# RWKV's input columns by halves of its heads, the memory's stage beside the weights, and mLSTM's denominators as columns

## The reference

```python
n = rmsnorm(x, attn_norm);  u = n @ w_in                 # 6928 columns of weights
mix = concat(gated_deltanet(u_gdn), mlstm(u_mlstm), rglru(u_rglru), rwkv7(u_rwkv))
x = x + mix @ w_out
n = rmsnorm(x, ffn_norm);   x = x + (silu(n @ w_gate) * (n @ w_up)) @ w_down
# second block: the normed memory of 256 tokens gives keys and values for one of three attentions
mem_n = rms_norm(mem, norm_mem_g);  mkv = mem_n @ w_mem_kv
x = x + merged_attentions(rms_norm(x) @ w_in_2, mkv) @ w_out_2;  return rms_norm(x, norm_final_g)
```

## Time and profile before

| | |
|---|---|
| median of three runs | 2525.97 us (2525.31 to 2526.02) |
| the profiled execution | 2521.66 us, span 2519.9 us |
| TensorE busy | 2442.4 us, 97%, 14420 matmuls |
| VectorE busy | 1438.4 us, 57%, 1852 instructions |
| ScalarE busy | 1131.4 us, 45%, 1408 instructions |
| POOL busy | 101.8 us, 4%, 93 instructions |
| TensorE's granted clock, mean | 0.986 of full speed |

### The profile page before, as it was taken

How to read it: one execution, slowest core, us unless ns; L and a number is a source line. 1 busy time by engine, 2 the same in 40 slices (tenths; PEclk the granted TensorE clock), 3 DMA queues, 4 the chain that set the end, 5 groups by cost and what they waited for, 6 DMA issues and landing times. The chain is left out here.

```text
span 2519.9 us, 34232 instructions
## 1 busy us (share of the span) xinstructions
PE 2442.4 (97%) x14420; PEld 2079.4 (83%) x14420; DVE 1438.4 (57%) x1852; ACT 1131.4 (45%) x1408; POOL 101.8 (4%) x93
## 2 busy tenths in 40 slices
PE   8999979998999999999999999999999999999998
PEld 8888878987788888888888887888888888888887
DVE  4575754776675555555555576545445655555554
ACT  5442622554354344444444464445544455344444
POOL 2000000121000000000000023000000000000000
PEclk9999989999999999999999999999999999999999
DMA  7633313644455555555556556555545544555564
GB/s 250 218 118 101 121 65 102 227 139 171 144 194 196 184 189 193 184 186 184 189 185 194 187 180 227 193 184 167 176 157 180 188 151 134 200 190 194 184 235 149
DMA packets 219528, 441.51 MB, mean 175 GB/s; under 512 B 11922, under 2 KB 15856, under 8 KB 216944
## 3 DMA queue, kind: packets, MB, share of 16 engines
q1 hardware_dynamic: 215632, 419.80, 50.4%
q0 software_dynamic: 3744, 19.53, 2.0%
HBM read 428.81 MB, written 10.49 MB: 174 GB/s over the span
## 5 line engine op out<-in xcount | busy, mean ns | idle before, releaser
L1183 ACT CAST ringH<-raw 128x1024 fp32r<-128x1024 f32 (+1 forms) x784 | 817.6, 1046 | 1060.2 <-PE ps L577 901.5
L1736 DVE TENSOR_TENSOR ringL<-raw,ringH 128x1024 fp32r<-128x1024 f32 (+1 forms) x784 | 951.7, 1231 | 431.0 <-ACT ringH L1183 429.9
L575 PE MATMUL ps<-ringH,nS 128*128 128x512 f32 x1376 | 554.2, 403 | 4.2 <-DVE ringL L1736 3.9
L576 PE MATMUL ps<-ringL,nS 128*128 128x512 f32 x1376 | 538.4, 391 | 0.0
L577 PE MATMUL ps<-ringH,nS 128*128 128x512 f32 x1376 | 538.4, 391 | 0.0
L603 PE MATMUL ps<-nS,ringH 128*128 128x256 f32 x1056 | 318.0, 301 | 16.5 <-DVE ringL L1736 16.5
L575 PEld LDWEIGHTS ps<-ringH,nS 128*128 128x128 f32 x1376 | 260.0, 189 | 58.6 <-issue 4.9
L604 PE MATMUL ps<-nS,ringH 128*128 128x256 f32 x1056 | 306.8, 291 | 0.0
L605 PE MATMUL ps<-nS,ringL 128*128 128x256 f32 x1056 | 306.5, 290 | 0.0
L577 PEld LDWEIGHTS ps<-ringH,nS 128*128 128x128 f32 x1376 | 259.5, 189 | 55.8
L576 PEld LDWEIGHTS ps<-ringL,nS 128*128 128x128 f32 x1376 | 260.4, 189 | 49.2
(11 more groups left out here) (392 smaller groups left out, 2175.4 us busy)
## 6 DMA issues: line engine op xcount, KB each, us to landing
raw<-in_w_in SPq DMA_DIRECT2D x187, 1024.0 KB, 5.1
raw<-in_ffn_w_gate SPq DMA_DIRECT2D x44, 1024.0 KB, 5.2
raw<-in_ffn_w_up SPq DMA_DIRECT2D x44, 1024.0 KB, 5.2
raw<-in_ffn_w_down SPq DMA_DIRECT2D x44, 1024.0 KB, 5.2
raw<-in_w_out SPq DMA_DIRECT2D x32, 1024.0 KB, 5.2
raw<-in_w_mem_kv SPq DMA_DIRECT2D x16, 1024.0 KB, 5.2
raw<-in_w_proj_a SPq DMA_DIRECT2D x8, 1024.0 KB, 5.2
raw<-in_w_proj_m SPq DMA_DIRECT2D x8, 1024.0 KB, 5.1
```

What stands on the lines that cost most here:

```text
L575: mm(o, XH[:, ts(j)], WH, first, False)
L576: mm(o, XH[:, ts(j)], WL, False, False)
L1183: e.copy(ringH[:, h % NSPL, 0:nh * cols], raw[:, u % NRAW, h0 * cols:(h0 + nh) * cols]).then_inc(*hi.tick(h))
L1736: tt2(ringL[:, h % NSPL, o], raw[:, u % NRAW, h0 * cols:(h0 + nh) * cols], ringH[:, h % NSPL, o].bitcast(F32), SUB).then_inc(*lo.tick(h))
```

## The change

- The `w` blocks become seven of 256 columns. `w0` to `w3` hold the first four heads' r, k, v and the low-rank columns, `w4` to `w6` the second four heads'. Units and half units still hold 2048 and 1024 columns, so a unit is then 8 k tiles. `weave` counts a step by its columns.
- `norm` places one step per pair instead of two.
- `mem` no longer stands by itself ahead of `rwkv`: a generator `beside_rwkv` runs it with four steps after each piece until `w3` is done, and the rest of it beside `rwkv`; `mlstm` follows in the same generator from `m3` on. ScalarE squares the memory's tokens after the second and third pair instead of behind the eighth. The buffer `memSt` becomes two tiles elsewhere, `memk` moves, and ScalarE's drain of `m0` waits for the squares and the four holding DMAs; POOL zeroes `mU` behind those DMAs.
- The token shift goes by pairs of tiles (one subtraction for two). The second heads' r, k and v are shifted inside the first heads' scan, after `Z` of chunks 0 to 2.
- Paces in `rwkv` and `gdn` are raised.
- mLSTM: `den` becomes one column per token and head, by six one-column matmuls in place of the product with `ones`; `m_t` is turned once for all heads. The absolute value, the MAX and the reciprocal work on columns, and the division moves into the factor of the norm.

The diff, cut to its core:

```diff
 def weave(self, stage, n):
         for pace in stage:
             due += n if pace is None else pace
-            self.step(int(due))
-            due -= int(due)
+            while self.i < len(self.steps) and due >= self.steps[self.i].block.cols / 512:
+                cost, i = self.steps[self.i].block.cols / 512, self.i
+                self.step()
+                due -= cost
+                if self.i == i:
+                    due = 0.0
+def beside_rwkv(L):
+    yield from L.stage("mem")
+    while not L.done("m3"):
+        yield
+    yield from L.stage("mlstm")
 def course(L):
-    L.weave(L.stage("norm"), 2)
+    L.weave(L.stage("norm"), 1)
...
-    L.weave(L.stage("mem"), 3)
-    L.weave(L.both(L.stage("rwkv"), L.stage("mlstm"), "m3"), 1.5)
+    side = beside_rwkv(L)
+    while not L.done("w3"):
+        next(side)
+        L.step(4)
+    L.weave(L.both(L.stage("rwkv"), side, "w3"), 1.5)
...
-        for q in range(4):
-            block(f"w{q}", win[:, RWC + 512 * q:min(RWC + 512 * q + 512, 6928)], 16, 512 if q < 3 else 256, "x", by="V")
+        for q in range(7):
+            c = RWC + (512 * q if q < 4 else 512 * (q - 4) + 256)
+            block(f"w{q}", win[:, c:c + 256], 16, 256, "x", by="V")
# TensorE, rwkv
-                for _ in range(7):
-                    yield 1.3
+                for _ in range(4):
+                    yield 2.5
...
# behind V's turn
-                    yield 4 + hh
+                    yield 6 + 2 * hh
# behind the spread of kk
-                    yield 3 + 3 * hh
+                    yield 4 + 4 * hh
# behind tokB
-                    yield 3 + hh
+                    yield 3 + 2 * hh
-                    yield from invert(rw_p, rw_v, rw_a, (hh, "inv"), narrow, GT, X, XR, T1, 5, 1.3 + 0.5 * hh)
+                    yield from invert(rw_p, rw_v, rw_a, (hh, "inv"), narrow, GT, X, XR, T1, 5, 1.5 + 0.8 * hh)
# TensorE, mlstm, per head
-                    for n in range(2):
-                        t = m1(b[:, 256 * n:256 * n + 256], ident[:, h:h + 1].broadcast_to([128, 128]), grows[3 + n], n == 0)
+                    t = m1(b[:, 0:256], ident[:, h:h + 1].broadcast_to([128, 128]), grows[3], True)
# m_t, turned once for all heads
+                    if h == 0:
+                        for tt in range(2):
+                            t = m1(b[:, 256 + 4 * tt:260 + 4 * tt], grows[4][:, ts(tt)], ident[:, 0:4], False)
...
-                    for n in range(2):
-                        for s in range(2):
-                            l_ = ones if n else mV[:, s, ts(h)]
-                            t = m1(b[:, 256 * n + 128 * s:256 * n + 256], l_, S_[:, s, 128 * s:256], n == 0 and s == 0)
+                    for s in range(2):
+                        mm(b[:, 128 * s:256], mV[:, s, ts(h)], S_[:, s, 128 * s:256], s == 0, False)
+                    for s, tt in ((0, 0), (0, 1), (1, 1)):
+                        for c in range(2):
+                            o = 128 * tt + 64 * c
+                            t = m1(b[half(c), 256 + tt:257 + tt], S_[:, s, o:o + 64], ones[:, 0:1], False)
# TensorE, gdn: paces 9 -> 10, 8 -> 9, 3.5 -> 4, inversion 2.6 -> 3
# ScalarE
# drain
+                if tag == "m0":
+                    e.wait_ge(*me_a.at("ss", 1))
+                    for g in range(4):
+                        e.wait_ge(s_mh[g], 16)
...
# mem, behind the eighth pair
-                square(0)
-                square(1)
...
-                    act(Mb, ring.of("ml", "H", h)[:, 256:512], ACT.Abs).then_inc(*ml_a.tick("ab", h))
# VectorE, rwkv
-                for k in [12, 13, *range(12)]:
...
+                for n, k in enumerate((12, 0, 4, 8)):
+                    shift(k, v3(SC + 512 * (n % 2), 2, T))
+                    yield
...
# in the scan, behind Z of chunk c
+                        if hh == 0 and c < 3:
+                            own(rw_v)
+                            shift(4 * c + 2, u3(4))
# VectorE, mlstm, per head
-                    tt2(Mb, Mb, Eb, MAX).then_inc(*ml_v.tick())
-                    e.reciprocal(Mb, Mb).then_inc(*ml_v.tick())
-                    tt2(Mb, Mb, mix[:, 4 + h, :], MUL).then_inc(*ml_v.tick())
-                    tt2(mix[:, 4 + h, :], Mb, b[:, 0:256], MUL).then_inc(*ml_v.tick("t3", h))
+                    tt2(mix[:, 4 + h, :], mix[:, 4 + h, :], b[:, 0:256], MUL).then_inc(*ml_v.tick())
+                    d = den[:, 2 * h:2 * h + 2]
+                    e.tensor_copy(d, b[:, 256:258]).then_inc(*ml_v.tick())
+                    stt(out=d, in0=d, scalar=-1.0, in1=d, op0=MUL, op1=MAX).then_inc(*ml_v.tick())
+                    tt2(d, d, low_m[:, 2 * h:2 * h + 2], MAX).then_inc(*ml_v.tick("t3", h))
```

More of the change, by code:

```diff
@@ L372, in program @@
         assert XBo >= 8704 and XBo + 4096 <= SC and SGo >= SC + 9728 + 2 * T + 512, (XBo, SC, NAR)
-        mSt = alias("memSt", SC + 4096, [128, 2, 4, 2, T])
+        assert MU + 988 == GU + 4096 and MU + 988 + 2048 <= RU
+        mSt = [alias(f"memSt{k}", o, [128, 4, 2, T]) for k, o in enumerate((0, MU + 988))]
         gateS = alias("gateS", 0, [128, 4096])
@@ L391, in program @@
         rxb, rmb = v2(SC + 9728, T), v2(SC + 9728 + T, T)
+        den, low_m, den_inv = (small[:, o:o + 8] for o in (64, 72, 80))
         col_rw, col_gd, col_ml = small[:, 24:32], small[:, 88:104], small[:, 104:112]
@@ L1000, in gdn @@
                         t.then_inc(*gd_p.tick("ga", w, g))
-                        yield 3.5
-                yield from invert(gd_p, gd_v, gd_a, ("inv",), wide, G8, X8, XR8, T8, 5, 2.6)
+                        yield 4
+                yield from invert(gd_p, gd_v, gd_a, ("inv",), wide, G8, X8, XR8, T8, 5, 3)
                 yield from join(gd_p, gd_v, ("inv",), G8, X8, XR8, T8, 2.6)
@@ L1289, in unit, with to_rows @@
                     place_rope(blocks[s.block.n - 1].tag)
-            def to_rows(key, mp, ma, gain, put, held, square):
+            def to_rows(key, mp, ma, gain, put, held, square, turns):
                 for n in range(8):
@@ L1298, in to_rows, with squared @@
                         act(put(k), ring.of(key, n)[:, 256 * j:256 * j + 256], ACT.Copy, scale=gain(k)).then_inc(*ma.tick("hi", k))
-                    if square and n == 0:
+                    if key == "nx" and n == 0:
                         high(0)
                         sent[0] = 1
-                    if square and n in (5, 6):
-                        square(n - 5)
+                    if n in turns:
+                        square(turns.index(n))
                     yield
-            def squared(ma, src, ss, landed):
+            def squared(ma, src, ss, landed, to):
                 def go(tt):
@@ L1388, in rwkv @@
                 L.upto("w3")
-                for g in range(4):
-                    e.wait_ge(s_mh[g], 16)
-                for _ in range(7):
+                for _ in range(4):
                     yield
@@ L1993, in rwkv @@
                 L.upto("w3")
-                for g in range(4):
-                    e.wait_ge(s_mh[g], 16)
                 e.wait_ge(*pool.at("wU"))
-                tmp = v3(SC, 4, T)
                 e.wait_ge(s_c, 48)
@@ L2574, in mem @@
                     e.wait_ge(*me_v.at("lo", 4 * g + 3))
[L2575 removed]
+                    e.dma_start(hm[:, 4 * g:4 * g + 4, :, :], mSt[g % 2][:, :, :, :].bitcast(F32)).then_inc(s_mh[g], 16)
                 e.wait_ge(*me_a.at("ss", 1))
+                for g in range(4):
+                    e.wait_ge(s_mh[g], 16)
+                e.memset(mU[:, :, 0:3], 0.0).then_inc(*pool.tick("mU"))
                 e.memset(gU[:, :, 0:3], 0.0).then_inc(*pool.tick("gU"))
@@ L2670, in xc @@
                 yield
-            course(lane(unit, {"norm": norm, "params": params, "gates": gates, "mem": mem, "gdn": gdn, "rglru": rglru, "gains": gains, "xf": finals, **{f"split2.{q}": split2(q) for q in range(4)}, "mk": mk, "mv": mv, "xc": xc}))
+            course(lane(unit, {"norm": norm, "params": params, "mem": mem, "gdn": gdn, "rglru": rglru, "gains": gains, "xf": finals, **{f"split2.{q}": split2(q) for q in range(4)}, "mk": mk, "mv": mv, "xc": xc}))
         def sync(e, S, ring, lane):
```

95 lines of the change are left out of this document (55 added, 40 removed).

## The result

The changed kernel takes 2499.74 us, median of four runs (2496.95 to 2501.49); the kernel before, run beside it, 2525.64 (2519.37 to 2526.02). The ratio is 0.9908, 95% interval 0.9894 to 0.9922: 25.9 us faster by the medians, 20 to 27 by the interval. The profiled execution has a span of 2497.1 us, 22.8 less than before; its first product of the split behind the output projection comes at 709.43 us, where it came at 733.63, so all of it is gained ahead of that point.

A forecast was written before the change was run, and what follows sets the result against it. TensorE's own work, plus idle time and lower clock, bounds the kernel. Terms -5, 2, 1.5, 9, 7, 2.6, 6, 2 gave 25 us off 2521.66, with 4.3 to the median: 2501 us (2488 to 2514; whole range 2479 to 2526).

The forecast's parts named there:

- Part 1: The start, up to the memory's factor: TensorE runs out of work under half steps; 5 us lost (1 to 10).
- Parts 2 and 3: Memory's stage, 2 us gained (0 to 3.6); RWKV's first half, 1.5 gained (2 lost to 4 gained).
- Parts 4 and 5: RWKV's second half and mLSTM: 9 us of idle time and 7 of clock gained; denominators: 2.6 of TensorE work gained.
- one long wait instead of five: RWKV's second half and mLSTM: fewer waits halve the lower clock's 14 us; 7 gained (0 to 12).
- Part 6: Gated DeltaNet: 6 us of idle time and 2 of clock gained; wait ahead of the inversion falls from 5.7 to 1.
- C: Rival, weights' loads: 256-column blocks fetched in 1 KB rows starve TensorE of weights; slower, 2535 us; chance 0.05.
- D: Rival: the halves are there but the count is wrong, so the stage begins where it did; 2528 us; chance 0.05.
- A: Rival: the second half's head waits 5 us or less and the clock stays up there; 2485 us; chance 0.20.
- B: Rival: VectorE's queue is late everywhere by as much as the paces give; 2525 us, no change; chance 0.13.

The follow-up runs named there:

- wide_first: Changed kernel with the same halves in blocks of 512 columns, two groups of 256 side by side, so the start has full steps: 2500.93 us, ratio 0.9917.
- Squares_last: Changed kernel with ScalarE's two squares of the memory's tokens back behind the eighth pair: 2507.37 us, ratio 0.9945.
- bank_early: Kernel before with one VectorE reordering: the product that reads H's bank goes first and the bank is given back there: 2507.61 us, ratio 0.9949.
- den_only: Kernel before with only the new mLSTM (denominators as columns), blocks and paces as they were: 2503.43 us, ratio 0.9922.
- den_undone: Changed kernel with the old mLSTM (product with ones, absolute value, MAX and reciprocal on 256 columns): 2522.59 us, ratio 1.0000.
- mask_first: Changed kernel with POOL's two products of gated DeltaNet's decay mask put ahead of RG-LRU's first product on POOL: 2504.33 us, ratio 0.9928.
- rg_late2: Changed kernel with two empty pieces ahead of RG-LRU, beside gated DeltaNet: 2505.34 us, ratio 0.9938.
- rg_late3: Changed kernel with three empty pieces ahead of RG-LRU, beside gated DeltaNet: 2502.78 us, ratio 0.9924.
- mask_gap: Changed kernel with POOL's decay mask first and one empty piece more behind RG-LRU's first gates on every engine: 2504.90 us, ratio 0.9932.
- conv_room: Changed kernel with six dense steps moved, in the second heads, from the inversion's levels to the gaps ahead of it: 2498.98 us, ratio 0.9914.
- rwkv_paces: Changed kernel with RWKV's four paces put back to those of the kernel before: 2507.89 us, ratio 0.9940.

## Why the prediction was right, and where it was not

The total came out (2499.7 for 2501), and the largest stage to the tenth; but two terms were wrong by 5 to 6 us in opposite directions, and that they cancel is luck. In the largest, most of the clock's share was given to the wrong edits.

**Part 1** held: factor at 30.81 us with seven full steps done (forecast 31), 4.6 us lost for 5. What the forecast did not see is that taking it back is worth nothing: wide_first had the start of the kernel before, and the time stayed. Its wait for `g2` came back, and the rest was lost in the first heads and in gated DeltaNet, for a reason that stays open.

```profile
30.81 0.71 PE L654 MATMUL ps<-cm,small 128*128 128x128 f32 x4 [3.00 <-DVE small L1889]
...
101.78 1.53 PE L799 MATMUL ps<-AR 128*128 128x256 f32 x6 [0.41 <-issue]
...
109.53 0.71 PE L654 MATMUL ps<-cm,small 128*128 128x128 f32 x4 [1.47 <-DVE small L1889]
```

**Parts 2 and 3** were mis-sized: 8.8 us for 3.5. The wait at the memory's factor is 1.47, as forecast; but `g2` waits 0.4 where the forecast left 2, and the lower clock in this stage (0.95, some 3.4 us) went altogether. The forecast had no clock term here, though the 4.9 us that it read up to 122 us lay partly in it. Squares_last shows that the early squares carry 5.5 of the 8.8: left behind the eighth pair, they stand ahead of `g2` on ScalarE.

**Parts 4 and 5** gave 18.6 for 18.6: 8.2 of idle time for 9, 8.9 of clock for 7, 2.2 of work for 2.6. (The pieces of the 9 add up to 7.8: 4.8 and 7 less the 4 by which the convolution's wait grows.) The forecast let the three waits for `t3` fall to 1 us by the shorter chain; that they wait for the bank which `t3` frees is the mechanism, and bank_early isolates it without a shorter chain. But it gave the 7 us of clock to "one long wait instead of five", of which the columns take only three; den_only, expected with 3 us of clock, gets 7.7 (14.1 to 6.4) with the old paces and the wait of 4.8 us for `ringL` still there. The convolution's wait came as worked out, 8.0 us for 9. It comes with the other edits (4.8 in bank_early, 2.4 in den_only, 8.0 in den_undone), and with the old divisions the second heads end up 5 us worse than before. VectorE's rows in the changed kernel (the first and the last of the four convolution steps, and what the inversion waits for):

```profile
275.90 2.95 DVE L2193 SCALAR_TENSOR_TENSOR AR<-AR,prm 128x256 f32<-128x256 f32 x6
...
289.43 2.96 DVE L2193 SCALAR_TENSOR_TENSOR AR<-AR,prm 128x256 f32<-128x256 f32 x6
...
294.20 0.69 DVE L1968 TENSOR_TENSOR AR<-AR 128x512 f32<-128x512 f32 x1
```

From 275.90 to 294.89 are 19.0 us, the 19 of the forecast. POOL's product fell ahead of them (272.46), not into them. The work on TensorE shrank by some 2.2 us, not 2.6: from start to start 0.43 instead of 0.87 for `MB` and 1.19 instead of 1.40 for H per head, less 0.36 for the turned column. The Trainium skill's page "TensorE: Matmul & The Clock Gate", section "Wait — 56ns, not 53.3ns?", gives about 25 ns as the floor from start to start of small matmuls, and 62 ns for each where hardware decode is off. The burst of twelve in 0.45 us (37 ns each) lies above the floor and is too fast for the 62.

**Part 6** failed: 1.6 for 8. The step that failed is "these now stand behind the inversion's first product, so I leave 1". They do stand there (at 570.66 us, the product at 551.76), and the wait is 7.0 us for 5.7 all the same. In the changed kernel VectorE stands 10 us for the decay mask, which POOL makes behind RG-LRU's product, and is then busy without a stop from 525 us to the inversion; in mask_first, rg_late2, rg_late3 and mask_gap it stands 6.1 to 7.2 us for ScalarE in RG-LRU's chain. That these stands cause the wait is argued from the order of the rows, not shown: four attempts moved them, none removed them, and the wait ahead of the inversion stayed at 6.2 us or more.

Of the rivals, C and D did not come. A's condition (the second heads' wait at 5 or less) came in conv_room, where 4.0 us of longer busy time took most of it, and in rwkv_paces, where three waits took its place. B's total came in den_undone, 0.3 us from no change: for the edits that the change is named after first, no change would have been right. B's mechanism, a late VectorE, fits there for the 5.0 us lost in the second heads, not for the 4.7 lost in the start.

## What to carry to other kernels

A change of many edits should be costed once for each edit made alone: here one edit gave 19 us, the others together nothing without it and some 4 to 7 with it (3.7 by the medians against den_only, whose intervals overlap, 6.7 by the table). Nor do edits taken out one at a time add up: the paces of RWKV alone, put back, cost some 8 us, and the place of the squares alone as much again. Look for a PSUM bank (or any buffer of a ring) that is held through work which no longer reads it: reordering three VectorE instructions gave 14 us. Dense work that covers waits is a fixed reserve; moving it to one wait takes it from another (with RWKV's paces put back, gated DeltaNet's wait rose from 7.0 to 10.2), so a new cover is worth only what the place it came from does not need.

## What was not expected of the hardware

In bank_early the lower clock had cost about as much as the waits. Three waits of 2.7 us taken away brought 7.2 us of idle time and 6.8 us of busy time for the same matmuls, which ran for longer at 2.4 GHz instead of 1.2. It is not a fixed price for a wait, however: conv_room shortened the longest wait by 6 us and the mean clock of the stage read lower, and the same instructions with the same idle time read 0.97 in one kernel and 0.95 in another. What sets it is left open.

The forecast put the dense record of 0.41 us at 15.2 us down to the lower clock, though the view reads 1.00 from 10 to 20 us. The traces bear the forecast out: their first record of the clock comes at 15.75 us in the kernel before, 15.24 in the changed one, 13.75 in bank_early and 13.25 in conv_room, the view takes the time ahead of it as full clock, and in each of the four the dense matmuls go at about that moment from one every 0.21 us to one every 0.12. Records of 0.41 us, 0.21 apart, are also what the kernel before shows in a stretch that reads 0.50:

```profile
64.00:70.00 6.00, 4.82 (x22) 4.82 (x23) 3.67 (x5) 1.72 (x2) 0.00 (x0) 0.50 0.62 207
...
66.41 0.41 PE L605 MATMUL ps<-nS,ringL 128*128 128x256 f32 x1
66.62 0.41 PE L603 MATMUL ps<-nS,ringH 128*128 128x256 f32 x1
```

So the clock's cost up to 122 us was more than the 4.9 us that the forecast read the earlier trace rows: the dense work from 10.1 to 15.75 us ran at half speed, an estimated 2.8 us, in the changed kernel 2.3.

POOL can slow VectorE by more than the forecast's 1.8 us: six 256-column operations took 7.88 us with two of POOL's products beside them in mask_first (POOL's took 2.40 and 2.60 us), 2.96 without. POOL's product of a block's rows took 6.02 us there, partly beside VectorE's subtractions for `ringL`, instead of 2.45.
